# The first layer's value weights in two chunks split by the contraction, with 512 columns moving per matmul

## The reference

```python
def diff_pool_layer(x, layer_idx, norm_g, w_in, q_g, k_g, lam_p, sub_g, w_group, pool_scale, w_out):
    proj = rms_norm(x, norm_g) @ w_in                      # 1024 -> 2048
    q, k, v, u = jnp.split(proj, [A_WIDTH, 2 * A_WIDTH, 3 * A_WIDTH], axis=-1)   # 512 each
    q = rms_norm(q.reshape(B, S, A_HEADS, 2, A_HEAD_DIM), q_g)
    k = rms_norm(k.reshape(B, S, A_HEADS, 2, A_HEAD_DIM), k_g)
    ...
    a_out = diff_attention(q, k, v, lam, lam_init, sub_g)  # 4 heads, two softmaxes each
    b_out = pool_mixer(u, w_group, pool_scale)             # 4 groups, window means
    mix = jnp.concatenate([a_out.astype(jnp.float32), b_out], axis=-1).astype(x.dtype)
    return x + mix @ w_out
```

## Time and profile before

| | us |
|---|---|
| median of 3 runs | 1034.45 (1033.99 to 1034.63) |
| profiled execution, own time | 1034.77 |
| its span, first to last instruction | 1033.0 |
| PE busy | 1008.0 (98%) |
| PE weight loads busy | 905.3 (88%) |
| DVE busy | 746.7 (72%) |
| ACT busy | 625.5 (61%) |
| POOL busy | 354.9 (34%) |

### The profile page before, as it was taken

The page is one execution under the profiler, slowest core; times in us unless marked ns, Lnnn a source line. Parts: engine busy times, 40 slices in busy tenths (PEclk is TensorE's granted clock), DMA queues, the critical chain, the costliest instruction groups (busy, mean ns, idle before and its releaser), DMA issues.

```text
span 1033.0 us, 15900 instructions
## 1 busy us (share of the span) xinstructions
PE 1008.0 (98%) x6476; PEld 905.3 (88%) x6476; DVE 746.7 (72%) x1009; ACT 625.5 (61%) x880; POOL 354.9 (34%) x189
## 2 busy tenths in 40 slices
PE   7999999999998899999999999999999899999997
PEld 7889988888987798888888888888999698888886
DVE  5886999874577779998548765654799887666543
ACT  6776677663377477766436555544669866455531
POOL 1062176640000025675102545510148223555300
PEclk9999999999999999999999999999999999999999
DMA  9533575537441335656553755556342247555441
GB/s 351 207 135 123 214 270 209 201 131 257 146 163 42 125 142 209 239 188 207 180 200 123 247 202 175 191 204 220 123 155 95 83 172 259 180 204 186 141 163 41
DMA packets 27143, 183.45 MB, mean 178 GB/s; under 512 B 3008, under 2 KB 3136, under 8 KB 5824
## 3 DMA queue, kind: packets, MB, share of 16 engines
q1 hardware_dynamic: 26496, 181.40, 49.2%
q10 hardware_dynamic: 576, 1.05, 0.3%
HBM read 181.39 MB, written 1.05 MB: 177 GB/s over the span
## 4 chain that ended last, share of the span: by engine, by line
PE 85%; DVE 6%; ACT 5%; issue 2%; POOL 1%; DMA 0%; DVEq 0%; POOLq 0%; ACTq 0%
PE psum L335 85%; DVE wlo L1564 2%; ACT whi L1030 1%; POOL Y L2246 1%; ACT Pb L1165 1%; DVE Pb L1696 1%; DVE Pb L1567 1%; DVE QK L1570 0%; DVE QR L1564 0%; DMA gain_x<-in_x 0%; DVE bias L1570 0%; ACT Ob L1373 0%; ACT PT L1030 0%; ACT sq L1156 0%; DVE st L1567 0%
## 5 line engine op out<-in xcount | busy, mean ns | idle before, releaser
L335 PE MATMUL psum<-G,whi 128*128 128x512 f32 (+1 forms) x1856 | 551.3, 359 | 6.5 <-DVE wlo L1564 6.5
L1564 DVE TENSOR_TENSOR wlo<-raw,whi 128x2048 fp32r<-128x2048 f32 (+1 forms) x170 | 386.9, 2291 | 177.6 <-ACT whi L1030 177.5
L335 PE MATMUL psum<-G,wlo 128*128 128x256 f32 x1568 | 442.9, 282 | 0.0
L1030 ACT ACTIVATE whi<-raw 128x2048 fp32r<-128x2048 f32 (+1 forms) x170 | 315.9, 1869 | 148.0 <-PE psum L335 136.3
L335 PEld LDWEIGHTS psum<-G,whi 128*128 128x128 f32 x1856 | 330.6, 189 | 59.1 <-DVE G L1570 6.4
L335 PEld LDWEIGHTS psum<-G,wlo 128*128 128x128 f32 x1568 | 298.0, 190 | 0.1
L335 PE MATMUL psum<-A2room,whi 128*128 128x512 f32 (+1 forms) x784 | 228.6, 355 | 0.0
L2246 POOL TENSOR_TENSOR A2room<-Ab,A2room 128x512 fp32r<-128x512 f32 x44 | 146.8, 3337 | 127.6 <-ACT A2room L1030 127.6
L335 PE MATMUL psum<-A2room,wlo 128*128 128x256 f32 x656 | 184.9, 282 | 0.0
L335 PEld LDWEIGHTS psum<-A2room,whi 128*128 128x128 f32 x784 | 138.3, 188 | 20.6
L2246 POOL TENSOR_TENSOR Ab<-Cb 128x512 f32<-128x512 f32 x44 | 109.6, 2491 | 107.7 <-ACT Cb L1073 107.1
(11 more groups left out here) (192 smaller groups left out, 1034.7 us busy)
## 6 DMA issues: line engine op xcount, KB each, us to landing
raw<-in_wst SPq DMA_DIRECT2D x165, 1024.0 KB, 4.9
bias<-in_bias_c SPq DMA_DIRECT2D x1, 2048.0 KB, 9.3
raw<-in_wst SPq DMA_DIRECT2D x3, 512.0 KB, 8.0
raw<-in_wst ACTq DMA_DIRECT2D x4, 256.0 KB, 6.3
out<-bias SPq DMA_DIRECT2D x4, 256.0 KB, 2.1
gain_x<-in_x SPq DMA_DIRECT2D x3, 256.0 KB, 6.5
bias<-in_bias_a SPq DMA_DIRECT2D x1, 512.0 KB, 7.9
bias<-in_invcnt SPq DMA_DIRECT2D x1, 512.0 KB, 6.8
```

What stands on the lines that cost most here:

```text
L335: return pe.matmul(o, a, b, start=start, stop=stop, skip_group_check=True)
L1030: return act.activation(o, i, ACT.Copy)
L1564: return dve.tensor_tensor(o, a, b, op)
```

## The change

The value weights are still two chunks, 6 and 7, of the same size. Now chunk 6 holds all 512 value columns over the first 512 rows of the contraction, chunk 7 the same columns over the last 512. The new `tokens_half(i, h)` makes 24 matmuls for a chunk, each with 512 weight columns moving: two token tiles by four contraction steps by three. Token tile 0 has bank 5 to itself and token tile 1 bank 4, so that both banks are open from the first half to the end of the second, and each is final only in the second. ACT's `take_v` gives way to `take_rows(t)`, one instruction of 512 columns for a token tile; the first waits for the new semaphore `s_vmm`, which PE raises when token tile 0 is final.

```diff
-    project("ab_w_in", (1536, 1664), (1792, 1920), (1024, 1152), (1280, 1408))
+    project("ab_w_in", (1536, 1664), (1792, 1920))
+    plan.append(("half", "ab_w_in", 1024, 0))
+    plan.append(("half", "ab_w_in", 1024, 4))
...
+            def tokens_half(i, h):
+
+                h3, l3 = weights(i, 4)
+                pe.wait_ge(s_lo, low_done(i))
+                for t in range(2):
+                    if h == 0:
+                        pe.wait_ge(s_u, t + 1)
+                    for j in range(4):
+                        k, xs = 4 * h + j, slice(t * P, t * P + P)
+                        last = three(bank[5 - t][:, :], Ghi[:, k, xs], Glo[:, k, xs], h3[:, j, :], l3[:, j, :], k == 0, k == DT - 1)
+                    if t == 0 and h == 1:
+                        last.then_inc(s_vmm, 1)
+                last.then_inc(s_used, 1)
...
                 def value(i):
-                    pe.wait_ge(s_vt, i // 2 + 1)
+                    pe.wait_ge(s_vt, 2)
...
-                pe.wait_ge(s_u, 1)
-                tokens_first(5, 6)
+                tokens_half(6, 0)
                 score(3)
-                pe.wait_ge(s_u, 2)
-                tokens_first(4, 7)
-                value(0)
+                tokens_half(7, 1)
                 pe.wait_ge(s_wg, 16)
                 pe.wait_ge(s_vt, 1)
                 mix_groups(0, 5)
                 turn(2)
+                value(0)
                 value(1)
...
+                def take_rows(t):
+                    act.wait_ge(s_rcol, 1)
+                    act.activation(Vt[:, t, :], bank[5 - t][:, :], ACT.Copy, scale=rcol[:, t:t + 1]).then_inc(s_vt, 1)
...
                 high(9)
-                act.wait_ge(s_used, USED[L0_CHUNK["v0"]])
-                take_v(0, 0, 5)
                 high(10)
                 exps(3, 0)
+                act.wait_ge(s_vmm, 1)
+                take_rows(0)
                 act.wait_ge(s_used, USED[L0_CHUNK["v1"]])
-                take_v(1, 1, 4)
+                take_rows(1)
+                group(0, 5)
                 take(0)
-                group(0, 5)
...
                 take_u(0)
+                take_u(1)
                 low(8)
                 bias_in(2)
-                take_u(1)
                 scale(3)
```

More of the change, by code:

```diff
@@ L266, in program @@
         s_lsum, s_lexp, s_lam, s_gsc, s_eps = sem("s_lsum"), sem("s_lexp"), sem("s_lam"), sem("s_gsc"), sem("s_eps")
+        s_vmm = sem("s_vmm")
         s_o, s_z, s_zln, s_zr, s_on, s_u, s_pool, s_mm, s_mmhi, s_upz = (
@@ L2420, in lay_out @@
             d[:, :, 128:256] = m8[:, :, c[3]:c[3] + 128].transpose(1, 0, 2)
+        elif c[0] == "half":
+            ws[i].reshape(P, 4, 512)[...] = m.reshape(8, P, m.shape[1])[c[3]:c[3] + 4, :, c[2]:c[2] + 512].transpose(1, 0, 2)
         elif c[0] == "heads":
```

## The result

| | us |
|---|---|
| before, median of 4 | 1034.54 (1033.99 to 1035.05) |
| changed, median of 4 | 1040.20 (1037.93 to 1041.05) |
| ratio | 1.0052, 95% interval 1.0040 to 1.0065 |
| changed, five more executions | 1037.29, 1037.52, 1039.55, 1040.38, 1040.82 |

The change makes the kernel 0.5% slower, 5.7 us, and not 0.25%, 2.7 us, as forecast; 1040.2 lies outside the range. The nine executions of the changed kernel fall into two groups: three from 1037.29 to 1037.93 with a mean granted TensorE clock of 0.997 to 0.998 over the whole execution, and six from 1039.55 to 1041.05 with 0.993 to 0.996. The kernel before, in the 61 executions beside the experiments, has 0.997 or 0.998 in all but one, which has 0.996. The mean is taken over a whole execution, so it tells that the clock fell somewhere, and only a trace tells where.

What follows compares the result with a forecast made beforehand. PE was taken as the bound, 85% of the chain and busy for 98% of the span. +2.66 us on its path took the profiled 1034.77 to 1037.4; less 0.32 for the median, 1037.1, range 1035.6 to 1038.4.

Steps and rivals of the forecast that it cites:

- The stream: PE's two value chunks: 8 triples of 0.68 us each instead of 16 of 0.355, saving 0.49 us together.
- The DVE slip: DVE idles for take_u(1)'s bank, so low(8) and the last head's exponentials start 1.05 us later.
- this case: DVE's low(8) may wait for a POOL instruction, up to 0.74 us, making the chain 3.4; not taken into the sum.
- ACT's order and the new hole: Both takes behind exps(3) on ACT, from 65.94; PE waits 2.8 us ahead of mix_groups(0), starting it at about 66.65.
- From there to `value(1)`, and behind it: PE from mix_groups(0): value(1) at 69.05 instead of 66.39, 2.66 us later; then 4.8 to the output projection, unchanged.
- third rival: TensorE's clock falls in the new hole: 24 matmuls cost 2.4 us more, 5.1 in all, 1039.5; chance 0.08.
- the late hole: Last attention: PE had 2.37 us idle and the rows behind kept full pace, taken as evidence against a clock fall.
- The range: 1035.6 to 1038.4 us, leaving out the clock, the empty wait and half of the tails of the other two.

Runs made afterwards that it cites:

- u_early: The kernel before with only take_u(1) moved ahead of low(8) and bias_in(2) on DVE: 1036.94 us, ratio 1.0021.
- again: The changed kernel itself once more, five executions beside the other experiments: median 1039.55 us, ratio 1.0049; its trace is of the execution of 1037.29.
- takes_first: The changed kernel with exps(3, 0) moved behind both take_rows in ACT's list: 1036.54 us, ratio 1.0023.
- u_back: The changed kernel with take_u(1) moved back behind bias_in(2) on DVE: 1036.99 us, ratio 1.0020.
- fill: The changed kernel with twelve more 512-column matmuls, read by nobody, into bank 3 right behind the value stream: 1037.69 us, ratio 1.0032.
- before_hole: The kernel before with one more wait on PE, value(0) waiting until the last head's softmaxes are combined: 1039.84 us, ratio 1.0056.

## Why the prediction was wrong, point by point

**The stream.** A triple of 512 columns took 0.70 us here (59.20 to 59.90), not the 0.68 of the earlier trace rows, so 0.08 us a chunk are saved (8 x 0.70 against 16 x 0.355), 0.16 in all and not 0.49. The saving was inside the wait anyway.

**The DVE slip.** Right in kind, too small. The idle time was as forecast, 0.38 against 0.45, but `low(8)` lost 0.4 us to POOL. The prediction named this case, with the Trainium skill's rule of the port lock ("SBUF — State Buffer", "SBUF: two separate sides") on its side, and left it out of the sum. What is shown is the coincidence of the two instructions, in seven traces against six. By the rule `low(8)` would wait for the 0.55 us that POOL's instruction still had to run, and it lost 0.41. With that 0.4 the slip is the 1.48 of u_early.

**ACT's order and the new hole.** Right in mechanism, and the hole, 2.85 us against 2.8, in part by luck. Counted from `blocks(3, 7)`, which frees the times from the shift at the start, the takes came 0.44 us later than forecast (15.35 against 14.91), for the longer `low(8)`. PE came to the hole 0.50 later (13.27 against 12.77), of which 0.33 is the saving that the stream didn't bring. Both ends moved alike, so the length came out.

**From there to `value(1)`, and behind it.** Right: 2.51 us from `mix_groups(0)` to `value(1)` with the clock held (66.66 to 69.17) against 2.40, then 4.80 to the output projection, as before. With `mix_groups(0)` 0.50 us later than forecast and 0.11 more from there, the waits add up to 3.27 instead of 2.66, and 3.26 were measured. The forecast of 1037.1 is near the executions with the clock held, 1037.29 to 1037.93, and that is partly luck too: in again `blocks(3, 7)` came 0.49 us earlier than in the kernel before (50.54 against 51.03), which hides most of the missing 0.6.

**The clock: the step that failed.** The prediction left the fall of TensorE's clock out of its sum; it had it as its third rival, at 0.08 and 2.4 us. It came in six of nine executions, which have a mean clock of 0.996 or less, and cost 3.5 us in the traced one. Two readings were wrong. The first was to take the one execution in which the late hole left the pace as it was for what such a hole does. The same stretch of the last attention, in the kernel before and in takes_first (the granted clock is the number behind the bracketed count):

```profile
806.00:812.00 6.00, 5.25 (x45) 1.00 0.16 30
```

```profile
806.00:812.00 6.00, 5.34 (x37) 0.72 0.00 1
```

So that hole, too, lets the clock fall in some executions, in seven of the thirteen traces; one trace shows one draw. At 0.65 to 2.09 us a fall it is also a likely reason for u_back's two groups, 1.4 us apart, but their slower group has no trace. The second was the price: 2.4 us, worked out from the 24 matmuls of the start, where 3.5 were measured. The clock stayed at 0.50 for at least 9.7 us, and there PE and ACT take turns, so that each longer matmul pushes the whole chain. The Trainium skill ("TensorE: Matmul & The Clock Gate", "What's actually happening") says that the throttled state is the default and that activity releases it. The runs agree as far as they go: in fill there was activity in the hole, and no execution fell. Why three of nine executions with the same hole kept the clock stays open.

**The range.** It ended at 1038.4 because the clock was left outside it. The forecast's sign was right, its size half.

## What to carry to other kernels

A hole in TensorE's stream is priced twice: by its length, and by the chance that the clock falls in it times what the work behind it then loses. Here a new 2.85 us hole cost 3.3 us with its waits and in two of three executions some 3 us more (2.8 between the groups' medians, 3.5 in the trace). Where a hole can't be closed, matmuls that nobody reads, put into a free bank, are a cheap cover and a clean test. And splitting a product by its contraction makes all of its outputs late together: look at who needed the first half early, and at what stands ahead of the two takes on their engine.

## What was not expected of the hardware

The fall is not a fixed property of the kernel. By their mean clocks 3 of 9 executions with the same 2.85 us hole kept 2.4 GHz; with 1.48 us none of 5 shows a clear fall, and with 3.41 us all 5 fell. In the changed kernel's trace the clock was down before the first matmul behind the hole (0.56 from 66.00 to 66.50, the hole ending at 66.88). In before_hole it fell only when PE was at work again, since 67.73: the granted clock is 1.00 from 67 to 68 us, 0.80 from 68 to 69 and 0.50 from 69 to 70.

A DVE instruction over two SBUF operands that starts 0.2 us into a POOL instruction took 2.70 instead of 2.29 us, and the next POOL instruction then 2.67 instead of 0.74, which it took before:

```profile
54.13 0.74 POOL L2246 TENSOR_TENSOR UP<-T,UP 128x256 f32<-128x256 f32 x1
```
